# Recurrent heads of a one-core transformer kernel: level products in adjacent pairs, a second pair of decay buffers, and a new order of work on three engines

## The chip, the cores and the metric

One Trainium2 core runs the whole program. The metric is the device time of one execution in microseconds. TensorE (PE) does the matrix products, VectorE (DVE) and ScalarE (ACT) the elementwise work, GpSimd (POOL) a part of it, SyncE (SP) issues the weight transfers.

## The reference

Two blocks follow each other on one sequence of 512 tokens and width 1024: a block of two attention layers, then one layer that mixes three branches and ends in a feed-forward part. The change lies in one branch of that mixing, four recurrent heads of 128 channels:

```
q = silu(q_raw) * 128**-0.5;  f = sigmoid(f_raw);  k = 1 - f;  v = i_in      (lb is zero here)
S_t = diag(f_t) S_{t-1} + k_t v_t^T          o_t = S_t^T q_t
o = rmsnorm(o) * w * silu(g_raw)
```

It is computed chunk by chunk. Beside it run a sparse attention branch (done before) and a causal depthwise convolution of 31 taps over 2 x 128 channels, followed by a layer norm over channels and a silu. The three results are multiplied by `w_out`; then come norm and feed-forward.

## The kernel before, in words

Everything is held transposed, 128 channels on the partitions and 512 tokens along the free axis. Each engine has its own program order, written out by hand; an engine runs its list in order and waits on semaphores. A projection is a "unit": a 1024x128 weight, split by ACT into a high part `wH` (L2278) and by POOL or DVE into a low part `wL` (L632), then eight tiles of three 512-column matmuls (L1068, L1069, L1070). These units fill PE between the small products of the heads.

The four heads t = 0 to 3 go through four windows. While head t is worked on, PE computes the units of gate and value for t and of forget and query for t+1 (`fill`, `gemm_h`), in the last window the output units (`output_m`). The unit index of the first output unit is UOM, and `split_h(n)` makes the high (ACT) or low (POOL) part of a unit a few ahead of PE.

Inside a 128-token chunk the decayed product of queries and keys is built from levels. DVE multiplies a running power of the decay onto queries and keys (`raise_q` L3188, then `raise_both(t, n)`, n = 1 to 7, L3196), each time on one half of the blocks of 2^(n-1) tokens, in place in one pair of rows of `kd` (`raised`). After each raise PE computes `product(t, p)`: 64x64 products of 128-deep queries and keys (L1900; p = 7 is L1896) into PSUM banks S[0] and T[1] in turn, and DVE merges them under a mask into `aT` (`joined(t, p)`, L3206 and L3207). `product(t, p)` with p over 2 waits for `joined(t, p - 2)`, and a raise waits for the product that reads what it overwrites.

Between heads: `turn_ke` transposes the keys (L1907), ACT copies them (`take_ke` L2622), `updates` makes the state updates (L1924), DVE chains them (`states_of` L3213, L3216), and `outputs` (L1933 with the merged products, L1937 with the states) gives the head's output in PSUM. `sum_h` (L1947) sums the squares that ACT takes (`square_h`); then `root_h` on ACT, `rooted_h`, `normed_h`, `gated_h`, `low_h` on DVE finish the head and split it for the output units.

The next head's start is a chain over three engines: ACT `queries(t)` (three functions on the query unit), DVE `queries_1`, ACT `silu_scalar_2(act, "hq", t, ...)` (L1087 on `kraw`), DVE `queries_2` (L3118), DVE `raise_q` (L3188), PE `product(t, 0)`. DVE must also have `clamped(t)` and `powers(t)` (L3173, L3180) behind it, which start from ACT's `factor(t)` (L2575).

The convolution's 62 terms are scaled by ACT (`terms`, L2499, three buffers) and added by POOL (`add_terms`, L670); each waits for the other. `CONV_HEAD` says how many pairs of them each window has. `conv_sum` on PE waits for the last one. While the heads finish, DVE also reduces four blocks of a modulation matrix (`ada_block`, L1185), two buffers deep: SP loads block n+2 once block n is reduced. They stand in DVE's list ahead of `rooted_h(3)`, and the last tile of the output units (`output_m(n, (3,))`) waits for `low_h(3)`:

```
silu_z(3)
blocks(0, 1)
states_of(3)
silu_vector_2(dve, "h", 3, zraw[:, :], zsig, mark("h_gated", 3))
blocks(1, 4)
rooted_h(3)
```

## Time and profile before

| | us |
|---|---|
| median of 3 runs (1186.29 to 1187.64) | 1187.64 |
| the profiled execution, its own time | 1187.51 |
| its span, first to last instruction | 1185.7 |

The profile gives for each engine its busy time and each instruction's start and length. A row of the timeline is start, length, engine, line, operation, output<-input, count, and in brackets the idle time before it with what ended it. The heads lie at 674 to 803 us of the span: head 0's first level product starts at 673.86, those of heads 1, 2 and 3 at 698.83, 731.14 and 768.60. The recorded length of a matmul includes its pipeline, so starts are compared, not ends.

### The profile page before, as it was taken

How to read it: one execution, taken by the hardware profiler on the slowest of the kernel's cores; microseconds unless marked ns; L12 is line 12 of the kernel's file. 1: busy time of each engine (PE TensorE's matmuls, PEld its weight loads, DVE VectorE, ACT ScalarE, POOL GpSimd, SP SyncE). 2: the span in 40 equal slices, each digit the busy share in tenths (PEclk: the TensorE clock that was granted, in tenths of full speed). 3: DMA queues.
4: the chain of work that ended last, by engine and by line, in shares of the span. 5: the costliest groups of instructions: out<-in, count | busy, mean ns of one | idle time of the engine just before them, and what ended most of it. 6: DMA issues, size and time to landing. Idle time of an engine off the chain costs nothing. (4 is left out here: it accounts for less than half of the span.)

```text
span 1185.7 us, 19704 instructions
## 1 busy us (share of the span) xinstructions
PE 1170.4 (99%) x7070; PEld 961.6 (81%) x7070; DVE 804.4 (68%) x1838; ACT 690.7 (58%) x1344; POOL 457.5 (39%) x300
## 2 busy tenths in 40 slices
PE   9999999999999999999999999999999999999998
PEld 8777777777877887789677777778988889899897
DVE  6867777775777877766589766886761375475575
ACT  6766676675546778734467888754541353443542
POOL 0301111112520000053477688315454577666663
PEclk9999999999999999999999999999999999999999
DMA  5423254451543323352322112333453324223322
GB/s 203 161 72 107 92 175 142 161 160 49 200 116 117 107 90 107 107 162 70 102 68 90 37 55 72 124 101 113 131 190 106 107 71 136 82 103 108 107 72 71
DMA packets 41041, 131.82 MB, mean 111 GB/s; under 512 B 4577, under 2 KB 7265, under 8 KB 40945
## 3 DMA queue, kind: packets, MB, share of 16 engines
q1 hardware_dynamic: 35360, 121.39, 32.0%
q10 hardware_dynamic: 5584, 9.18, 2.4%
q8 instruction: 57, 0.93, 0.3%
q14 instruction: 40, 0.32, 0.1%
HBM read 127.10 MB, written 2.13 MB: 109 GB/s over the span
## 5 line engine op out<-in xcount | busy, mean ns | idle before, releaser
L1068 PE MATMUL G<-hi,wH 128*128 128x512 f32 x1032 | 417.3, 404 | 1.1 <-DVE qkv L3118 0.5
L1070 PE MATMUL G<-hi,wL 128*128 128x512 f32 x1032 | 403.1, 391 | 0.0
L1069 PE MATMUL G<-lo,wH 128*128 128x512 f32 x1032 | 402.4, 390 | 0.0
L632 POOL TENSOR_TENSOR wL<-w,wH 128x1024 fp32r<-128x1024 f32 x89 | 220.3, 2483 | 431.7 <-ACT wH L2278 428.4
L1068 PEld LDWEIGHTS G<-hi,wH 128*128 128x128 f32 x1032 | 193.8, 188 | 56.2 <-issue 17.9
L1070 PEld LDWEIGHTS G<-hi,wL 128*128 128x128 f32 x1032 | 193.7, 188 | 42.1
L1069 PEld LDWEIGHTS G<-lo,wH 128*128 128x128 f32 x1032 | 194.1, 188 | 38.3 <-issue 1.9
L2278 ACT ACTIVATE wH<-w 128x1024 fp32r<-128x1024 f32 x140 | 147.2, 1054 | 105.3 <-DMA w<-weights_dram 56.1
L417 POOL TENSOR_TENSOR kd<-kd,band 128x256 f32<-128x256 f32 x8 | 6.4, 796 | 192.8 <-DMA kd<-c_dram 192.8
L2852 DVE TENSOR_TENSOR wL<-w,wH 128x1024 fp32r<-128x1024 f32 x51 | 62.3, 1221 | 15.5 <-ACT wH L2278 15.4
L1185 DVE CUSTOM_DVE_ANT_0 adaw<-adaw,scr 128x1024 f32<-128x1024 f32 x36 | 62.5, 1737 | 0.0
L1222 ACT ACTIVATE scr<-scr,sa 128x256 f32<-128x256 f32 (+2 forms) x64 | 35.2, 557 | 22.7 <-DVE sa L1209 22.7
L2744 ACT ACTIVATE pieceH<-O 128x512 fp32r<-128x512 f32 x22 | 13.2, 599 | 58.0 <-DVE N L3389 38.0
L2779 ACT ACTIVATE relu<-G 128x512 f32<-128x512 f32 x24 | 14.3, 597 | 49.4 <-PE G L1070 49.4
L2125 PE MATMUL G<-sumH,pieceL 128*128 128x256 f32 x132 | 37.4, 283 | 0.0
L2123 PE MATMUL G<-sumH,pieceH 128*128 128x256 f32 x132 | 37.4, 283 | 0.0
L2124 PE MATMUL G<-sumL,pieceH 128*128 128x256 f32 x132 | 37.3, 283 | 0.0
L3408 DVE SCALAR_TENSOR_TENSOR xT<-G,modT,xT 128x256 f32<-128x256 f32 x44 | 21.2, 481 | 22.3 <-PE G L2125 22.1
L3196 DVE TENSOR_TENSOR kd<-kd,S 128x512 f32<-128x512 f32 x28 | 19.2, 686 | 23.9 <-PE T L1900 13.0
L710 POOL TENSOR_TENSOR pieceL<-wp,pieceH 128x512 fp32r<-128x512 f32 x18 | 25.3, 1408 | 11.8 <-ACT pieceH L2744 11.4
L1139 DVE TENSOR_TENSOR sg<-zraw,th 128x512 f32<-128x512 f32 x16 | 11.1, 692 | 26.4 <-ACT th L1087 26.4
L1245 ACT ACTIVATE scr<-T 128x384 f32<-128x384 f32 (+1 forms) x48 | 22.6, 522 | 10.9 <-PE T L1234 10.2
(565 smaller groups left out, 2569.6 us busy)
## 6 DMA issues: line engine op xcount, KB each, us to landing
w<-weights_dram SPq DMA_DIRECT2D x150, 512.0 KB, 3.6
adaw<-ada_dram SPq DMA_DIRECT2D x48, 512.0 KB, 4.4
wp<-weights_dram SPq DMA_DIRECT2D x20, 512.0 KB, 4.4
kd<-c_dram ACTq DMA_DIRECT2D x16, 512.0 KB, 5.2
xT<-x_dram SPq DMA_DIRECT2D x4, 512.0 KB, 8.1
out_dram<-xT SPq DMA_DIRECT2D x8, 256.0 KB, 2.2
scr<-ca_dram SPq DMA_DIRECT2D x2, 512.0 KB, 6.1
kd<-cbias SPq DMA_DIRECT2D x8, 128.0 KB, 4.3
```

Source lines behind the costliest of these rows:

```text
L632: g.tensor_tensor(wL[:, u.slot], raw_home(u), wH[:, u.slot].bitcast(f32), ALU.subtract).then_inc(w_lo, 1)
L710: g.tensor_tensor(pieceL[:, piece(q, i)], home, pieceH[:, piece(q, i)].bitcast(f32), ALU.subtract).then_inc(piece_lo_g, 1)
L1068: mm(home[:, :], whi, H[:, k, :], start=(k == first), stop=False)
L1069: mm(home[:, :], whi, L[:, k, :], start=False, stop=False)
L1070: last = mm(home[:, :], wlo, H[:, k, :], start=False, stop=(k == final))
L1185: v.tensor_tensor_reduce(out=home, in0=home, in1=copy, scale=1.0, scalar=0.0, op0=ALU.mult, op1=ALU.add, accum_out=modsum[:, b.n:b.n + 1]) ...
L1222: s.activation(part, part, ACT.Exp, bias=sa[:, n % 2, LOW, h, q:q + 1], scale=-1.0, accum_out=sa[:, n % 2, ASUM, h, q:q + 1]).then_inc(sem ...
L2123: mm(home, pieceH[:, at, k, :], high, start=first and k == 0, stop=False, skip_group_check=True)
L2124: mm(home, pieceH[:, at, k, :], low, start=False, stop=False, skip_group_check=True)
L2125: last = mm(home, pieceL[:, at, k, :], high, start=False, stop=(k == 3), skip_group_check=True)
L2278: s.activation(wH[:, u.slot], raw_home(u), ACT.Copy).then_inc(w_hi, 1)
L2852: v.tensor_tensor(wL[:, u.slot], w32[:, u.slot % 2], wH[:, u.slot].bitcast(f32), ALU.subtract).then_inc(w_lo, 1)
```

## The change

- Level products 3 and 4, and 5 and 6, stand next to each other in PE's list, with all of the filling between the pairs; `turn_ke(t)` follows `product(t, 7)` directly instead of opening the next window.
- `raised(t, n)` gives a second pair of rows of `kd` for n = 4, 5 and 8. The raise that goes from one pair to the other writes only its half of the blocks; ACT copies the other half (`leave(t, n)` for n = 3, 5, 7, twelve copies in all). Products 4 and 6, raises 4 and 6 and `turn_ke` wait for these copies; raises 3, 5 and 7 no longer wait for a product.
- The convolution's pairs are 3, 8, 4, 0 instead of 4, 8, 3, 0. On ACT, one pair of each window's terms is put between `queries(t)` and the query's sigmoid for t = 1 and 2.
- DVE does `states_of(t - 1)` before `queries_1(t)`, and `states_of(3)` before `silu_z(3)` and the first modulation block. The last window has a list of its own on ACT and DVE. The two `conv_scaled` of head 2's window move into head 3's.

```diff
--- before.py
+++ after.py
-CONV_HEAD = [4, 8, 3, 0]
+CONV_HEAD = [3, 8, 4, 0]
...
+AFTER.update({"h_moved": ("c_here0", 64)})
...
-def raised(t):
-
-    return kd[:, 2 - 2 * (t % 2), :], kd[:, 3 - 2 * (t % 2), :]
-
-def moved_on(t, m):
-
-    q = raised(t)[0]
+def raised(t, n):
+
+    row = 2 - 2 * (t % 2) + (4 if n in (4, 5, 8) else 0)
+    return kd[:, row, :], kd[:, row + 1, :]
+
+def moved_on(t, m, n):
+
+    q = raised(t, n)[0]
     return bass.AP(q.tensor, q.offset + m, [list(q.ap[0]), [SEQ - m, 2], [2 * m, SEQ // (2 * m)], [1, m]])
+
+def left_behind(t, m, n):
+
+    q = raised(t, n)[0]
+    return bass.AP(q.tensor, q.offset, [list(q.ap[0]), [SEQ + m, 2], [2 * m, SEQ // (2 * m)], [1, m]])
...
+        if p in (4, 6):
+            pe.wait_ge(*mark("h_moved", 3 * t + p // 2 - 1))
...
         gemm_h(1, 0, (3, 4))
         product(0, 2)
         turn_h(0)
-        gemm_h(1, 0, (5,))
+        gemm_h(1, 0, (5, 6, 7))
         product(0, 3)
-        gemm_h(1, 0, (6, 7))
         product(0, 4)
-        gemm_h(1, 1, (0, 1))
+        gemm_h(1, 1, (0, 1, 2, 3))
         product(0, 5)
-        gemm_h(1, 1, (2, 3))
         product(0, 6)
-        gemm_h(1, 1, (4, 5))
+        gemm_h(1, 1, (4, 5, 6))
         product(0, 7)
-        gemm_h(1, 1, (6, 7))
+        turn_ke(0)
+        gemm_h(1, 1, (7,))
 
     def opened(t):
 
-        turn_ke(t - 1)
         fill(t, 0)
         updates(t - 1)
         fill(t, 1)
...
 
         opened(t)
         fill(t, 3)
+        fill(t, 4, (0, 1))
         product(t, 3)
+        product(t, 4)
         if t == 2:
             conv_sum()
-        fill(t, 4)
-        product(t, 4)
+        fill(t, 4, (2, 3))
         fill(t, 5)
         product(t, 5)
+        product(t, 6)
         if t == 2:
             conv_sqsum()
         fill(t, 6)
-        product(t, 6)
         fill(t, 7, (0, 1))
         product(t, 7)
+        turn_ke(t)
         fill(t, 7, (2, 3))
 
     def last_window():
 
         opened(3)
-        fill(3, 3, (0, 1))
+        fill(3, 3)
         product(3, 3)
-        fill(3, 3, (2, 3))
         product(3, 4)
         output_m(0, (4, 5))
+        output_m(1, (4, 5))
         product(3, 5)
-        output_m(1, (4, 5))
         product(3, 6)
         output_m(0, (0, 1))
+        output_m(1, (0, 1))
         product(3, 7)
-        output_m(1, (0, 1))
         turn_ke(3)
...
+    def leave(t, n):
+
+        m = 1 << (n - 1)
+        act.wait_ge(sem("h_x"), 8 * t + n + since("h_x"))
+        if n == 3 and t > 1:
+            act.wait_ge(sem("h_o"), t - 1 + since("h_o"))
+        s.activation(left_behind(t, m, n + 1), left_behind(t, m, n), ACT.Copy).then_inc(sem("h_moved"), 1)
...
+        leave(0, 3)
         take_hv(0)
         gate_1(0)
         conv_terms(0, 0)
-        split_h(4)
+        leave(0, 5)
         forget(1)
         conv_terms(0, 1)
-        conv_terms(0, 2)
-        conv_terms(0, 3)
+        split_h(4)
+        leave(0, 7)
+        factor(1)
+        take_first(0)
+        take_ke(0)
+        keys(1)
         take_blocks(0)
-        take_first(0)
-        keys(1)
-        factor(1)
         silu_scalar_2(act, "h", 0, zsig)
 
     def window(t):
-        take_ke(t - 1)
         queries(t)
-        if t == 1:
-            split_h(5)
+        conv_terms(t - 1, 2 if t == 1 else 7)
+        split_h(4 * t + 1)
         split_h(4 * t + 2)
         silu_scalar_2(act, "hq", t, kraw[:, :])
         conv_terms(t, 0)
         raw_h(t, 2, vraw, sem("h_vturn"), t + since("h_vturn"))
-        if t == 3:
-            for k in range(2):
-                act.wait_ge(sem("conv_z"), k + 1)
-                silu_scalar_1(act, link, "cv", k, cacc[:, k, :], cv_th[k])
         conv_terms(t, 1)
         square_h(t - 1)
         conv_terms(t, 2)
-        if t == 3:
-            for k in range(2):
-                silu_scalar_2(act, "cv", k, cv_th[k])
-            for k in range(2):
-                act.wait_ge(sem("cv_gated"), k + 1)
-                s.activation(hi1[:, 6 + k, :], cv_th[k], ACT.Copy).then_inc(sem("cv_gated_hi"), 1)
+        leave(t, 3)
         conv_terms(t, 3)
         take_hv(t)
         root_h(t - 1)
         conv_terms(t, 4)
         raw_h(t, 3, zraw, sem("h_silu"), t + since("h_silu"))
         gate_1(t)
+        leave(t, 5)
         conv_terms(t, 5)
         split_h(4 * t + 3)
         if t == 2:
             for k in range(2):
                 act.wait_ge(sem("conv_centred"), k + 1)
                 s.activation(csq[:, k, :], cacc[:, k, :], ACT.Square).then_inc(sem("conv_sq"), 1)
+        forget(t + 1)
+        leave(t, 7)
+        split_h(4 * t + 4)
         gated_h(t - 1)
-        if t < 3:
-            forget(t + 1)
-        split_h(4 * t + 4)
-        if t < 3:
-            silu_scalar_2(act, "h", t, zsig)
+        silu_scalar_2(act, "h", t, zsig)
         conv_terms(t, 6)
         if t == 2:
             act.wait_ge(sem("conv_sqsum"), 1)
             rsqrt_scalar(link, 1, 1.0 / 256, sem("conv_var"), sem("conv_root"))
-        if t < 3:
-            keys(t + 1)
-            factor(t + 1)
+        factor(t + 1)
+        take_first(t)
+        take_ke(t)
+        keys(t + 1)
         take_blocks(t)
-        take_first(t)
-        conv_terms(t, 7)
-        if t < 3:
-            split_h(4 * t + 5)
+
+    def conv_gate_1(k):
+        act.wait_ge(sem("conv_z"), k + 1)
+        silu_scalar_1(act, link, "cv", k, cacc[:, k, :], cv_th[k])
+
+    def last_window():
+        queries(3)
+        split_h(13)
+        split_h(14)
+        silu_scalar_2(act, "hq", 3, kraw[:, :])
+        raw_h(3, 2, vraw, sem("h_vturn"), 3 + since("h_vturn"))
+        conv_gate_1(0)
+        square_h(2)
+        conv_gate_1(1)
+        leave(3, 3)
+        take_hv(3)
+        root_h(2)
+        raw_h(3, 3, zraw, sem("h_silu"), 3 + since("h_silu"))
+        for k in range(2):
+            silu_scalar_2(act, "cv", k, cv_th[k])
+        leave(3, 5)
+        for k in range(2):
+            act.wait_ge(sem("cv_gated"), k + 1)
+            s.activation(hi1[:, 6 + k, :], cv_th[k], ACT.Copy).then_inc(sem("cv_gated_hi"), 1)
+        gate_1(3)
+        split_h(15)
+        leave(3, 7)
+        take_first(3)
+        take_ke(3)
+        take_blocks(3)
+        gated_h(2)
+        split_h(16)
 
     attend_c()
     first_window()
-    for t in range(1, 4):
+    for t in range(1, 3):
         window(t)
-    take_ke(3)
+    last_window()
...
-        dve.wait_ge(sem("h_products"), 8 * t + (2 if n == 1 else n + 1) + since("h_products"))
+        if n in (1, 2, 4, 6):
+            dve.wait_ge(sem("h_products"), 8 * t + (2 if n == 1 else n + 1) + since("h_products"))
+        if n in (4, 6):
+            dve.wait_ge(*mark("h_moved", 3 * t + n // 2 - 1))
         dve.wait_ge(sem("h_x"), 8 * t + n + since("h_x"))
         by = power(m).rearrange("p (n a) -> p a n", a=2).unsqueeze(3).broadcast_to((P, 2, SEQ // (2 * m), m))
-        v.tensor_tensor(moved_on(t, m), moved_on(t, m), by, ALU.mult).then_inc(sem("h_x"), 1)
+        v.tensor_tensor(moved_on(t, m, n + 1), moved_on(t, m, n), by, ALU.mult).then_inc(sem("h_x"), 1)
...
-        level_of(0, 2)
+        raise_both(0, 2)
+        raise_both(0, 3)
+        joined(0, 2)
         low_c(dve, 0)
-        level_of(0, 3)
+        raise_both(0, 4)
+        joined(0, 3)
+        raise_both(0, 5)
+        joined(0, 4)
+        gates(1)
+        raise_both(0, 6)
+        raise_both(0, 7)
+        joined(0, 5)
+        joined(0, 6)
         low_c(dve, 1)
-        for n in range(4, 7):
-            level_of(0, n)
-        raise_both(0, 7)
-        gates(1)
         silu_z(0)
 
     def conv_root():
...
         for b in range(first, last_):
             ada_block(dve, Block(ADA_OM, b), 48)
 
-    def window(t):
+    def opened(t):
         clamped(t)
         powers(t)
+        states_of(t - 1)
         queries_1(t)
-        states_of(t - 1)
         queries_2(t)
         raise_q(t)
         silu_vector_2(dve, "h", t - 1, zraw[:, :], zsig,
                       mark("h_gated", t - 1) if t > 1 else (sem("a_gated_lo"), 10))
+        if t == 3:
+            conv_scaled(0)
         raise_both(t, 1)
         joined(t, 0)
         joined(t, 1)
         if t == 3:
-            for k in range(2):
-                silu_vector_1(dve, "cv", k, cacc[:, k, :], cv_th[k])
-        level_of(t, 2)
-        if t == 3:
-            conv_gate()
-        level_of(t, 3)
-        if t == 3:
-            conv_low()
-            level_of(t, 4)
+            conv_scaled(1)
+        raise_both(t, 2)
+        raise_both(t, 3)
+        joined(t, 2)
+
+    def window(t):
+        opened(t)
         rooted_h(t - 1)
-        if t < 3:
-            normed_h(t - 1)
+        raise_both(t, 4)
+        joined(t, 3)
         if t == 2:
             conv_centre()
-        level_of(t, 5 if t == 3 else 4)
-        if t == 3:
-            normed_h(t - 1)
+        raise_both(t, 5)
+        joined(t, 4)
+        normed_h(t - 1)
+        silu_z(t)
+        raise_both(t, 6)
+        raise_both(t, 7)
+        joined(t, 5)
+        joined(t, 6)
         gated_h(t - 1)
-        if t < 3:
-            silu_z(t)
-        level_of(t, 6 if t == 3 else 5)
+        gates(t + 1)
         low_h(t - 1)
-        if t < 3:
-            gates(t + 1)
-            level_of(t, 6)
         if t == 2:
             conv_root()
-        raise_both(t, 7)
-        if t == 2:
-            for k in range(2):
-                conv_scaled(k)
+
+    def last_window():
+        opened(3)
+        for k in range(2):
+            silu_vector_1(dve, "cv", k, cacc[:, k, :], cv_th[k])
+        raise_both(3, 4)
+        joined(3, 3)
+        raise_both(3, 5)
+        joined(3, 4)
+        conv_gate()
+        rooted_h(2)
+        raise_both(3, 6)
+        joined(3, 5)
+        raise_both(3, 7)
+        conv_low()
+        joined(3, 6)
+        normed_h(2)
+        gated_h(2)
+        low_h(2)
 
     logits_c(dve, 4)
     logits_c(dve, 5)
...
     gate_c(dve, 0)
     gate_c(dve, 1)
     first_window()
-    for t in range(1, 4):
+    for t in range(1, 3):
         window(t)
+    last_window()
+    states_of(3)
     silu_z(3)
     blocks(0, 1)
-    states_of(3)
     silu_vector_2(dve, "h", 3, zraw[:, :], zsig, mark("h_gated", 3))
     blocks(1, 4)
     rooted_h(3)
```

## Rows read from the trace of the kernel before

**Rows 1.** The page: span and busy time of PE.
```profile
span 1185.7 us, 19704 instructions
...
PE 1170.4 (99%) x7070; PEld 961.6 (81%) x7070; DVE 804.4 (68%) x1838; ACT 690.7 (58%) x1344; POOL 457.5 (39%) x300
```

**Rows 2.** Busy time by stretch: length, PE, PEld, DVE, ACT, POOL, clock, DMA.
```profile
707.00:728.50 21.50, 21.44 (x154) 16.48 (x153) 14.50 (x31) 21.14 (x37) 19.40 (x14) 1.00 0.17 50
731.00:768.60 37.60, 35.83 (x255) 26.80 (x254) 26.10 (x54) 25.84 (x43) 17.12 (x11) 1.00 0.37 121
```

**Rows 3.** Timeline of PE around one level product between filling matmuls.
```profile
707.35 0.39 PE L1070 MATMUL G<-hi,wL 128*128 128x512 f32 x1
707.67 0.69 PE L1900 MATMUL T<-kd 128*64 128x64 f32 x16
708.28 0.50 PE L1068 MATMUL G<-hi,wH 128*128 128x512 f32 x1
708.62 0.39 PE L1069 MATMUL G<-lo,wH 128*128 128x512 f32 x1
```

**Rows 4.** Timeline of PE at the starts of heads 1 to 3 and later.
```profile
696.61 1.05 PE L1933 MATMUL O<-scr,qkv 128*128 128x128 f32 x8
...
698.83 0.69 PE L1900 MATMUL T<-kd 128*64 128x64 f32 x16 [0.50 <-DVE kd L3188]
...
731.14 0.69 PE L1900 MATMUL T<-kd 128*64 128x64 f32 x16
...
740.59 1.98 PE L1953 MATMUL N<-tmp,ones 128*128 128x512 f32 x4
...
764.88 1.05 PE L1933 MATMUL O<-scr,qkv 128*128 128x128 f32 x8
...
768.60 0.69 PE L1900 MATMUL T<-kd 128*64 128x64 f32 x16 [0.45 <-DVE kd L3188]
...
770.02 0.39 PE L1069 MATMUL G<-lo,wH 128*128 128x512 f32 x1
...
790.79 1.05 PE L1933 MATMUL O<-scr,qkv 128*128 128x128 f32 x8
...
792.27 0.48 PE L1068 MATMUL S<-hi,wH 128*128 128x512 f32 x1
...
802.35 0.40 PE L1068 MATMUL G<-hi,wH 128*128 128x512 f32 x1
```

**Rows 5.** Timeline of ACT: both query sigmoids, and the value copy of head 1.
```profile
696.64 0.61 ACT L1087 ACTIVATE kraw<-kraw 128x512 f32<-128x512 f32 x1
...
707.04 0.58 ACT L2640 ACTIVATE qkv<-T 128x512 f32<-128x512 f32 x1
...
728.45 0.61 ACT L1087 ACTIVATE kraw<-kraw 128x512 f32<-128x512 f32 x1
```

**Rows 6.** Timeline of POOL: two low splits, the last addition, one low split.
```profile
726.55 4.78 POOL L632 TENSOR_TENSOR wL<-w,wH 128x1024 fp32r<-128x1024 f32 x2
...
737.17 1.28 POOL L670 TENSOR_TENSOR tmp<-tmp,sq 128x511 f32<-128x511 f32 x1
...
785.50 2.39 POOL L632 TENSOR_TENSOR wL<-w,wH 128x1024 fp32r<-128x1024 f32 x1 [0.35 <-ACT wH L2278]
```

**Rows 7.** Timeline of DVE from the gate of head 3 to its low part.
```profile
786.22 2.22 DVE L1082 SCALAR_TENSOR_TENSOR scr<-zraw,scr 128x512 f32<-128x512 f32 x1
788.37 1.22 DVE L1185 CUSTOM_DVE_ANT_0 adaw<-adaw,scr 128x1024 f32<-128x1024 f32 x1
...
791.18 1.22 DVE L1185 CUSTOM_DVE_ANT_0 adaw<-adaw,scr 128x1024 f32<-128x1024 f32 x1
...
796.69 1.23 DVE L1185 CUSTOM_DVE_ANT_0 adaw<-adaw,scr 128x1024 f32<-128x1024 f32 x1
...
797.84 0.69 DVE L781 SCALAR_TENSOR_TENSOR sq<-sq,scr 128x512 f32<-128x512 f32 x1
...
801.45 0.69 DVE L3233 TENSOR_TENSOR lo<-O,hi 128x512 fp32r<-128x512 f32 x1 [0.67 <-ACT hi L2617]
```

More of the change, by code:

```diff
@@ L1891, in product @@
                     pe.wait_ge(sem("h_aT"), 7 * t + p - 1 + since("h_aT"))
-                q, k = raised(t)
+                q, k = raised(t, max(p, 1))
                 out_ = half_of(p)
@@ L1904, in turn_ke @@
                 pe.wait_ge(sem("h_x"), 8 * t + 8 + since("h_x"))
+                pe.wait_ge(*mark("h_moved", 3 * t + 3))
                 pe.wait_ge(sem("h_v"), t + 1 + since("h_v"))
                 for c in range(3):
-                    last = nc.tensor.transpose(T[0][:, c * P:(c + 1) * P], raised(t)[1][:, c * P:(c + 1) * P], ident[:, :])
+                    last = nc.tensor.transpose(T[0][:, c * P:(c + 1) * P], raised(t, 8)[1][:, c * P:(c + 1) * P], ident[:, :])
                 last.then_inc(sem("h_keT"), 1)
@@ L1936, in outputs @@
                 for c in range(1, NQ):
-                    last = mm(O[:, c * P:(c + 1) * P], state[:, c - 1, :], raised(t)[0][:, c * P:(c + 1) * P], start=False,
+                    last = mm(O[:, c * P:(c + 1) * P], state[:, c - 1, :], raised(t, 8)[0][:, c * P:(c + 1) * P], start=False,
                               stop=(c == NQ - 1))
@@ L2593, in keys @@
                     act.wait_ge(sem("h_keT"), t - 1)
-                s.activation(raised(t)[1], klog, ACT.Exp, scale=-1.0).then_inc(sem("h_k"), 1)
+                s.activation(raised(t, 1)[1], klog, ACT.Exp, scale=-1.0).then_inc(sem("h_k"), 1)
             def queries(t):
@@ L3187, in raise_q @@
                     dve.wait_ge(sem("h_o"), t - 1 + since("h_o"))
-                v.tensor_tensor(raised(t)[0], power(1), hq, ALU.mult).then_inc(sem("h_x"), 1)
+                v.tensor_tensor(raised(t, 1)[0], power(1), hq, ALU.mult).then_inc(sem("h_x"), 1)
             def raise_both(t, n):
                 m = 1 << (n - 1)
-                dve.wait_ge(sem("h_products"), 8 * t + (2 if n == 1 else n + 1) + since("h_products"))
+                if n in (1, 2, 4, 6):
+                    dve.wait_ge(sem("h_products"), 8 * t + (2 if n == 1 else n + 1) + since("h_products"))
+                if n in (4, 6):
+                    dve.wait_ge(*mark("h_moved", 3 * t + n // 2 - 1))
                 dve.wait_ge(sem("h_x"), 8 * t + n + since("h_x"))
                 by = power(m).rearrange("p (n a) -> p a n", a=2).unsqueeze(3).broadcast_to((P, 2, SEQ // (2 * m), m))
-                v.tensor_tensor(moved_on(t, m), moved_on(t, m), by, ALU.mult).then_inc(sem("h_x"), 1)
+                v.tensor_tensor(moved_on(t, m, n + 1), moved_on(t, m, n), by, ALU.mult).then_inc(sem("h_x"), 1)
             def joined(t, p):
```

## The prediction

> **What bounds the kernel now.** I read the page first: PE is busy 1170.4 of 1185.7 us [rows 1], so only PE's order and its few idle stretches can be worth anything, and the whole kernel has about 15 us of idle PE. Next the timeline of PE through the heads, from start to start. It is one unbroken stream of filling matmuls with small work between, with gaps mainly where a new head opens [rows 4]: from the start of the merged-product outputs to the first level product 2.22 us pass for head 1 and 3.72 us for head 3, while the same stretch of the last head, where nothing waits, takes 1.48 us. The stall is 0.7 us at head 1 and 2.2 us at head 3. Then ACT: between its value copy of head 1 and the query sigmoid of head 2 it is busy 21.14 of 21.50 us [rows 2, 5]. In that window ACT, not PE, has no room. In the next one (731 to 768.6) ACT is busy only 25.8 of 37.6 us. Last the tail: the tile of the output units that needs the last head starts at 802.35 [rows 4], and the low part that it needs was begun at 801.45 and takes 0.69 us [rows 7], so it ended at 802.14. PE arrives there just as it is ready. Any earlier arrival of PE is worth nothing unless that chain comes earlier too.
>
> **Adjacent products.** PE gets no instruction more or less. A lone product costs 708.62 - 707.35 = 1.27 us from filling matmul to the second one after it; two filling steps of 0.23 us would have passed anyway, which leaves 0.81 us [rows 3]. The pair of head 3 takes 1.42 us from its start to the second filling matmul [rows 4]; less one step of 0.23, plus the 0.09 of entry that the lone one shows, 1.28 us. A merge saves 0.34 us. There are eight, 2.7 us; the transposes beside product 7 I put at under 0.1 us each. With the two stalls above and some tenths at head 1's transposes the ceiling is some 6 to 7 us, if nothing new waits.
>
> **The copies on ACT.** No row shows one. The nearest is the same engine's 128x512 from SBUF to SBUF, 0.61 us [rows 5]; as they read and write in steps it could be more, but hardly over twice that, and because consecutive instructions overlap by a tenth it could be 0.5. I take 0.6. In the first window they and one dropped pair of terms nearly cancel (three copies 1.8, a pair 1.2), so head 1 opens near 698.3, and ACT's value copy of head 1 stays at about 707.1, since before it ACT and POOL pace each other through the convolution terms and POOL's list is no shorter. From there to the query sigmoid of head 2 is 728.45 - 707.04 = 21.4 us of solid work. The new order has the same work there (the pair of terms and the high splits of the next units stand in front of the sigmoid in both) and two copies more: 707.15 + 21.4 + 1.2 = 729.75. From the sigmoid to product 0 it takes 698.83 - 696.64 = 2.2 us (head 2 took 2.7) [rows 4, 5]. Product 0 of head 2 comes at 732.0, against 731.14: 0.8 us later, though PE could be there at about 729.6. What the merges of two windows gave, and the stalls of the first, turns into a wait for the query chain. Behind it on PE stands everything else.
>
> **Head 2's window.** Product 0 to product 0 of head 3 was 37.46 us. Off go the stall 2.24 and two merges 0.7: `conv_scaled` (two operations per half) no longer stands ahead of the powers on DVE, and the states come ahead of the queries. On comes a wait for the convolution: POOL does one pair of terms more ahead of its two low splits, which began at 726.55 [rows 6] and now follow the terms that ACT computes only after `queries(2)`, so about 729.6; after them come two additions of up to 1.28 more. The last addition ended at 738.45 and will end at 738.45 + 3.1 + 2 x 1.28 = 744.1. `conv_sum` stood at 740.59; it moves by 0.8, six filling steps (1.4) and a second product (0.5) to 743.3, and waits 0.8. Head 3 opens at 732.0 + 37.46 - 2.24 - 0.7 + 0.8 = 767.3, against 768.60. If ACT or POOL are quicker than I think, 766.
>
> **The last window and its tail.** PE saves two merges more and would reach the last tile at 802.35 - 1.3 - 0.7 = 800.3. But the tail is later. DVE's new list ends with raise 6, joined 5, raise 7, two `conv_low`, joined 6, `normed_h(2)`, `gated_h(2)`; `rooted_h(2)` holds raise 6 to about 782.0, and with steps of 0.6 (0.35 for a joined, 0.8 and 0.7 for the last two) `gated_h(2)` ends at 786.6. ACT's high copy takes 0.6, `low_h(2)` 0.6, and then `states_of(3)` 1.05 stands ahead of the gate: `silu_z(3)` is due at 788.9. ACT goes from that high copy into the high split of 16 (1.04 us) and POOL's low split follows, about 788.2 to 790.6. This is the moment that decides. In the trace `silu_z(3)` took 2.22 us and ended at 788.44, 0.55 us after the low split that ran on POOL from 785.50 to 787.89 [rows 6, 7]; both its inputs are in SBUF. So it is held again, to 791.2. The first modulation block starts at 791.1 instead of 788.37. From its start to the end of the second were 4.03 us, now 2.95, as the states no longer lie between: 794.05 instead of 792.40. SP may load the fourth only then, and it takes 4.29 us to be there (796.69 - 792.40): 798.35; 1.15 us on, `rooted_h(3)` starts at 799.5 instead of 797.84. Its chain to the low part is unchanged, so the last tile starts at about 804.0, 1.7 us later than before, with PE idle for some 3.7 us in front of it. Behind 803 us everything follows that tile.
>
> The Trainium skill, "SBUF — State Buffer", section Who interferes with whom, says that a VectorE instruction with two inputs in SBUF and a GpSimd instruction that reads SBUF exclude each other, and the one that comes second waits for the whole of the first. By that rule, which the 2.22 us agree with, the gate is held; without it the first block starts at 789.5, `rooted_h(3)` at 797.9, and the sum is no change.
>
> **The sum.** The profiled execution took 1187.51 us for its span of 1185.7, 0.1 from the median of 1187.64. Heads 0 and 1 +0.8, head 2's window -2.1, last window -0.7, tail +3.7: 1.7 us, so 1187.64 + 1.7 = 1189.3 us. A measurement of this kernel can tell about 0.2%, 2.4 us, from no change.
>
> **Rivals.**
> - *A second hold in the last window (slower).* `conv_low(1)`, whose inputs are both in SBUF, is due at 784.1; the low split of 15 starts on POOL at 784.1 too (`conv_gate` done 780.6, then copy 0.5, gate 1.85, split 1.04). If POOL is first, DVE loses 2.3 us; `output_m(0, (6, 7))` on PE waits for it and the tail starts 2.3 later: 1191.6 us. It decides from one or two tenths on. For it: the tie. Against it: a tenth of delay on ACT undoes it. Chance 0.20.
> - *The gate is not held (no change).* If the low split of 16 starts after 788.9 or is over, the tail comes as before, 1187.7 us. Against it: both times hang on the same high copy and lie 0.7 us apart. Chance 0.15.
> - *PE's arrival decides (faster).* If the low part of the last head is ready by 800.3, the gain is 2.0 us, 1185.6; without the wait for `conv_sum` and with head 2's sigmoid a microsecond sooner, 1183.8. For it: the two stalls do go. Against it: the chain of two buffers of 4.3 us per load is in DVE's list ahead of `rooted_h(3)` in both kernels. It needs the first block to start by 787.4. Chance 0.23.
> - My forecast, 0.42.
>
> **How the numbers follow.** The forecast's own range is 1.7 +- 1 us, as window 2 can come out 1.3 us earlier and a copy can cost 0.5 to 1 us: 1188.3 to 1190.5. A quarter of it lies over 2.4 us. Slower by over 0.2%: 0.20 + 0.10 = 0.30. Faster by over 0.2%: three quarters of the third rival, 0.18. The rest 0.52 within. The range runs from the third rival's far end to the first's: 1184.0 to 1191.8; I leave out 0.1 on either side.
>
> **What the profile after would show.** Products 3 and 4, 5 and 6 with 0.5 us from start to start; twelve copies on ACT of about 0.6; product 0 of head 2 not earlier than 731 with an idle PE in front of it, released by DVE's raise; product 0 of head 3 near 767.3; no stall on the states; `conv_sum` behind POOL's last addition; `silu_z(3)` over 2 us long; a PE idle for 2 to 4 us before the last tile, behind `low_h(3)`. I am wrong if head 2 opens at 730 (then ACT had room), if head 3 opens before 765.5, or if the last tile starts within 0.5 us of 800.3.

## The result, and the profile after

The changed kernel takes 1190.22 us (median of 11 runs, 1188.25 to 1193.19) against 1187.64 for the kernel before (11 runs, 1184.55 to 1189.97): ratio over all runs 1.003, 95% interval 1.002 to 1.0041 (the two medians alone give 1.0022). Forecast were 1189.3. It is slower, in the direction of the forecast: by 2.6 us between the medians where 1.7 were forecast, and by some 3.6 us, twice the forecast, by the ratio.

The page of the changed kernel, next to [rows 1]: PE has 3.3 us less busy time in a span that is 2.6 us longer.

```profile
span 1188.3 us, 19706 instructions
...
PE 1167.1 (98%) x7070; PEld 961.0 (81%) x7070; DVE 803.2 (68%) x1838; ACT 695.7 (59%) x1356; POOL 458.9 (39%) x300
```

The best single reading is one window, from head 0's first level product to the start of the last tile. Columns as in [rows 2]. First the kernel before:

```profile
673.86:802.35 128.49, 125.94 (x959) 96.56 (x959) 92.05 (x192) 95.16 (x158) 72.67 (x48) 1.00 0.27 83
```

then the changed one:

```profile
673.44:804.81 131.37, 122.70 (x959) 96.63 (x959) 91.12 (x192) 100.39 (x170) 73.07 (x48) 1.00 0.25 81
...
707.15:729.93 22.78, 22.03 (x162) 17.81 (x161) 14.85 (x32) 22.45 (x38) 17.57 (x13) 1.00 0.16 47
732.11:767.70 35.59, 34.92 (x254) 26.75 (x254) 22.20 (x49) 27.28 (x46) 21.16 (x14) 1.00 0.32 108
```

PE does the same 959 matmuls in 3.24 us less busy time. That is what PE's new order gives, the adjacent products foremost (no run takes them apart from the rest of the order). Its idle time in the stretch goes from 128.49 - 125.94 = 2.55 us to 8.67. So 6.12 us of new idle time stand against 3.24 us of gain: 2.88 us longer. From the last tile on, both kernels are alike: 383.35 us to the end of the span before, 383.49 after. The start of the stretch lies anywhere from 670.5 to 673.9 us in the twelve profiled executions, one of each kernel, for reasons that lie ahead of the heads. So from here on I count from head 0's first product.

Where the idle time is, timeline of PE:

```profile
698.37 0.69 PE L1909 MATMUL T<-kd 128*64 128x64 f32 x16 [1.64 <-DVE kd L3226]
...
703.97 1.12 PE L1957 MATMUL N<-sq,ones 128*128 128x512 f32 x2 [0.26 <-ACT sq L2618]
...
709.15 0.69 PE L1909 MATMUL T<-kd 128*64 128x64 f32 x16
709.66 0.64 PE L1909 MATMUL S<-kd 128*64 128x64 f32 x16
710.23 0.50 PE L1075 MATMUL G<-hi,wH 128*128 128x512 f32 x1
710.57 0.39 PE L1076 MATMUL G<-lo,wH 128*128 128x512 f32 x1
...
716.66 0.50 PE L1075 MATMUL G<-hi,wH 128*128 128x512 f32 x1 [0.60 <-DVE scr L1089]
...
732.11 0.69 PE L1909 MATMUL T<-kd 128*64 128x64 f32 x16 [0.92 <-DVE kd L3226]
...
744.42 1.98 PE L1963 MATMUL N<-tmp,ones 128*128 128x512 f32 x4 [0.32 <-POOL tmp L677]
...
767.70 0.69 PE L1909 MATMUL T<-kd 128*64 128x64 f32 x16
...
792.91 1.13 PE L1957 MATMUL N<-sq,ones 128*128 128x512 f32 x2 [1.48 <-ACT sq L2618]
...
804.81 0.50 PE L1075 MATMUL G<-hi,wH 128*128 128x512 f32 x1 [2.59 <-DVE lo L3274]
```

Read the brackets against [rows 4]. All brackets of the stretch, with three that are not shown (0.35, 0.16 and 0.35), add up to the 8.67 us. The pair (709.15, 709.66) costs 1.42 us to the second filling matmul, as forecast. The stalls ahead of head 3 (1.28 on the states, in the row of the kernel before below, and 0.45 on the raise) are gone. New are 1.64 ahead of head 1 (was 0.50), 0.60 on DVE's gate at 716.66, 0.92 ahead of head 2 (was none), 1.48 at `sum_h(3)` and 2.59 at the last tile.

```profile
767.22 0.94 PE L1937 MATMUL O<-kd,scr 128*128 128x128 f32 x6 [1.28 <-DVE scr L3216]
```

ACT ahead of head 2 (compare [rows 5]): the copy, the value copy of head 1, two high splits, the query's sigmoid.

```profile
705.58 0.62 ACT L2639 ACTIVATE kd<-kd 128x512 f32<-128x512 f32 x1
...
707.63 0.58 ACT L2657 ACTIVATE qkv<-T 128x512 f32<-128x512 f32 x1
...
728.04 1.99 ACT L2287 ACTIVATE wH<-w 128x1024 fp32r<-128x1024 f32 x2
729.93 0.61 ACT L1094 ACTIVATE kraw<-kraw 128x512 f32<-128x512 f32 x1
```

POOL in the windows of heads 2 and 3 (compare [rows 6]):

```profile
730.09 5.17 POOL L639 TENSOR_TENSOR wL<-w,wH 128x1024 fp32r<-128x1024 f32 x2
...
743.10 1.27 POOL L677 TENSOR_TENSOR tmp<-tmp,sq 128x511 f32<-128x511 f32 x1
...
784.45 2.90 POOL L639 TENSOR_TENSOR wL<-w,wH 128x1024 fp32r<-128x1024 f32 x1 [16.09 <-ACT wH L2287]
788.80 2.36 POOL L639 TENSOR_TENSOR wL<-w,wH 128x1024 fp32r<-128x1024 f32 x1 [1.45 <-ACT wH L2287]
```

DVE in the tail (compare [rows 7]): second `conv_low`, `silu_z(3)`, the four blocks, `rooted_h(3)`, `low_h(3)`.

```profile
784.42 0.69 DVE L3304 TENSOR_TENSOR lo<-rinv,hi 128x512 fp32r<-128x512 f32 x1
...
789.24 2.47 DVE L1089 SCALAR_TENSOR_TENSOR scr<-zraw,scr 128x512 f32<-128x512 f32 x1
791.64 1.21 DVE L1192 CUSTOM_DVE_ANT_0 adaw<-adaw,scr 128x1024 f32<-128x1024 f32 x1
...
793.39 1.21 DVE L1192 CUSTOM_DVE_ANT_0 adaw<-adaw,scr 128x1024 f32<-128x1024 f32 x1
...
797.87 1.22 DVE L1192 CUSTOM_DVE_ANT_0 adaw<-adaw,scr 128x1024 f32<-128x1024 f32 x1
...
799.31 1.23 DVE L1192 CUSTOM_DVE_ANT_0 adaw<-adaw,scr 128x1024 f32<-128x1024 f32 x1
...
800.46 0.69 DVE L788 SCALAR_TENSOR_TENSOR sq<-sq,scr 128x512 f32<-128x512 f32 x1
...
804.06 0.69 DVE L3274 TENSOR_TENSOR lo<-O,hi 128x512 fp32r<-128x512 f32 x1 [0.66 <-ACT hi L2626]
```

Put the last two fences beside each other. POOL starts the low split of unit 16 at 788.80, DVE starts the gate at 789.24, and the gate ends 2.47 us later, at 791.71, half a microsecond after the split (791.16). The earlier pair is the near miss of the second rival: DVE started `conv_low(1)` at 784.42, POOL its split at 784.45. DVE was first by 0.03 us, ran its normal 0.69, and POOL took 2.90 in place of 2.36 to 2.41.

### The profile page after: what moved, and what is told of

It is laid out like the page before. It is cut to its first block, busy times and chain, and to the rows that moved or that the text cites. A ratio compares the mean times of both kernels' runs of the same rounds, so it can differ in the third digit from the quotient of the medians.

```text
span 1188.3 us, 19706 instructions
## 1 busy us (share of the span) xinstructions
PE 1167.1 (98%) x7070; PEld 961.0 (81%) x7070; DVE 803.2 (68%) x1838; ACT 695.7 (59%) x1356; POOL 458.9 (39%) x300
## 4 chain that ended last, share of the span: by engine, by line
PE 54%; DVE 7%; issue 7%; POOL 3%; ACT 2%; DMA 2%; SPq 0%; ACTq 0%; DVEq 0%; POOLq 0%
PE G L1075 10%; PE G L1077 10%; PE G L1076 10%; DMA adaw<-ada_dram 2%; PE G L2132 2%; PE G L2134 2%; PE G L2133 2%; POOL wL L639 2%; DVE best L3202 1%; DVE adaw L3204 1%; PE S L1426 1%; PE T L1473 1%; PE O L1489 1%; POOL pieceL L717 1%; POOL tmp L677 1%
## 5 line engine op out<-in xcount | busy, mean ns | idle before, releaser
L3471 DVE SCALAR_TENSOR_TENSOR xT<-G,modT,xT 128x256 f32<-128x256 f32 x44 | 21.2, 482 | 22.3 <-PE G L2134 22.0
L1216 DVE CUSTOM_DVE_ANT_0 scr<-S,kd 128x256 f32<-128x256 f32 (+2 forms) x64 | 28.5, 487 | 0.0
```

## The experiments

Ten kernels ran. Each number in the table is from the one profiled execution of its kernel and counts from head 0's first product (those of `e1` and `e9` were the slowest of all runs of their kernel, that of `e2` the fastest); "idle" is PE's idle time right before the last tile, "rest" the time from that tile's start to the end of the span.

| kernel | head 1 | head 2 | head 3 | last tile | idle | rest |
|---|---|---|---|---|---|---|
| before | 24.97 | 57.28 | 94.74 | 128.49 | 0 | 383.4 |
| changed | 24.93 | 58.67 | 94.26 | 131.37 | 2.59 | 383.5 |
| e1_tail_order | 24.94 | 58.67 | 94.26 | 133.07 | 0 | 383.2 |
| e2_gate_early | 24.94 | 58.68 | 94.27 | 130.77 | 3.44 | 383.4 |
| e3_copies_twice | 24.94 | 60.35 | 96.50 | 133.79 | 2.75 | 384.9 |
| e4_sigmoid_earlier | 24.26 | 57.73 | 94.28 | 131.16 | 2.35 | 383.5 |
| e5_blocks_early | 24.92 | 58.66 | 94.27 | 127.15 | 0 | 383.3 |
| e6_before_blocks_early | 24.99 | 57.31 | 94.80 | 128.57 | 0 | 383.3 |
| e7_both | 24.26 | 57.73 | 94.26 | 127.99 | 0 | 383.6 |
| e8_conv_sum_later | 24.25 | 57.72 | 93.92 | 127.66 | 0 | 383.3 |
| e9_split_16_short | 24.92 | 58.66 | 94.25 | 130.22 | 2.91 | 385.1 |
| e10_windows_1_2 | 24.23 | 57.70 | 93.89 | 126.81 | 0 | 383.6 |

### e1: the tail's order as before

```diff
     last_window()
-    states_of(3)
     silu_z(3)
     blocks(0, 1)
+    states_of(3)
```

> The changed kernel with the gate of head 3 and the first modulation block ahead of states_of(3), as before. My theory (the tail decides: the gate is held behind POOL's low split): the gate is issued before POOL starts, takes 0.7 instead of 2.47 us, the first block starts 2.7 us earlier, the outputs of head 3 wait 1.3 us for the states, the fourth block lands 1.6 us earlier and the last tile of the output units starts 1.6 us earlier. Total about 1188.6 us, 0.13% under the changed kernel. Rival (the tail is set by PE's arrival or by the transfers alone): no change from the changed kernel, 1190.2.

Measured 1189.58 us, ratio 1.0025 (1.0015 to 1.0036). The gate was indeed not held (0.68 us), but what came next was. All engines, in order of time:

```profile
788.24 0.68 DVE L1089 SCALAR_TENSOR_TENSOR scr<-zraw,scr 128x512 f32<-128x512 f32 x1
788.76 2.37 POOL L639 TENSOR_TENSOR wL<-w,wH 128x1024 fp32r<-128x1024 f32 x1 [1.45 <-ACT wH L2287]
788.85 3.37 DVE L1192 CUSTOM_DVE_ANT_0 adaw<-adaw,scr 128x1024 f32<-128x1024 f32 x1
```

The first block takes 3.37 us for 1.21. The states behind it are late, and PE waits 3.22 us for them:

```profile
793.25 1.65 PE L1947 MATMUL O<-kd,scr 128*128 128x128 f32 x6 [3.22 <-DVE scr L3257]
```

TensorE's granted clock falls to 0.50 of full speed within that wait, at about 792 us, and stays there until 799; filling matmuls start every 0.42 us in place of 0.23. The last tile is 1.7 us later than in the changed kernel. The last head's low part on DVE and the tile on PE tell what of this is the tail:

```profile
804.49 0.69 DVE L3274 TENSOR_TENSOR lo<-O,hi 128x512 fp32r<-128x512 f32 x1 [0.67 <-ACT hi L2626]
...
806.47 0.39 PE L1075 MATMUL G<-hi,wH 128*128 128x512 f32 x1
```

Counted from head 0 the low part starts at 131.09, 0.47 us later than in the changed kernel (130.62). The other 1.2 us are PE, which comes after the low part is ready: from the outputs with the states to the tile it takes 13.22 us, and in the changed kernel, without its two waits, 10.84. So some 2.4 us are the low clock. My expectation was wrong: the hold had moved to another instruction, and the tail was no shorter for it. One order keeps the states early and the gate held, the other frees the gate and holds the block. Without the low clock PE would have been at the tile before the low part, and the tile some 0.5 us later and not 1.7. The times of all runs do not show the loss: the ratio is 1.0025 here and 1.003 for the changed kernel.

### e2: the gate ahead of `low_h(2)`

```diff
     gated_h(2)
+    silu_z(3)
     low_h(2)
     ...
     states_of(3)
-    silu_z(3)
```

> The changed kernel with silu_z(3) between gated_h(2) and low_h(2), where DVE is idle for 0.8 us. My theory: the gate takes 0.7 us, states_of(3) keep their time, the first block starts 2.4 us earlier, and the last tile too: PE idle in front of it falls from 2.6 us to about 0.3. Total about 1187.8 us, level with the kernel before. Rival (the loads of the blocks decide, and they stand on SP behind the load that waits for POOL's low split of 16, at 791.2): the third block lands no earlier than 795.6 and the fourth with it, and the gain is 1 us or less. Rival (PE's arrival decides): no gain.

Measured 1189.53 us, 1.0025 (1.0015 to 1.0036). The gate, at 783.82, takes 1.15 us. Again the hold passes on, all engines:

```profile
785.86 2.37 POOL L639 TENSOR_TENSOR wL<-w,wH 128x1024 fp32r<-128x1024 f32 x1 [1.45 <-ACT wH L2287]
786.45 2.86 DVE L1192 CUSTOM_DVE_ANT_0 adaw<-adaw,scr 128x1024 f32<-128x1024 f32 x1
```

The first block ends 0.6 us earlier than in the changed kernel (counted from head 0), and so does the last tile. The gate started 2.5 us earlier, and only 0.6 of it was left once block 0 had met the split. PE's idle time before the tile rose to 3.44 us where I had expected 0.3, since PE no longer waits at `sum_h(3)` and comes sooner.

### e3: three copies of head 1 done twice

```diff
     s.activation(left_behind(t, m, n + 1), left_behind(t, m, n), ACT.Copy)
+    if t == 1:
+        link(s.activation(left_behind(t, m, n + 1), left_behind(t, m, n), ACT.Copy))
```

> The changed kernel with each of the three copies of head 1 done twice on ACT, the second after the first has ended (about 0.65 us each). My theory (ACT has no room in head 1's window): two of the three extra copies lie behind the value copy, and product 0 of head 2 comes 1.3 us later, with PE idle in front of it; head 3 and the last tile follow by about the same, 1.3 us, total 1191.5. Rival (the copies are hidden in ACT's idle time): no change in the place of product 0 of head 2.

Measured 1192.65 us, 1.0048 (1.0031 to 1.0065). A second copy takes 0.65 us, and three of them move head 2 by 1.68 us, head 3 by 2.24, the last tile by 2.42. Two of them, 1.3 us, lie behind the value copy, which itself comes 0.4 us later. ACT has no room before head 2, and what is lost there is not won back. The further 0.56 us at head 3 are not the copies alone: behind the 2.23 us that PE waits ahead of head 2 the granted clock is 0.50 from 734 to 737.5 us, which this expectation did not foresee.

### e4: the query's sigmoid ahead of the second high split

```diff
     split_h(4 * t + 1)
-    split_h(4 * t + 2)
     silu_scalar_2(act, "hq", t, kraw[:, :])
+    split_h(4 * t + 2)
```

> The changed kernel with the query sigmoid of heads 1 and 2 ahead of the second of the two high splits on ACT. My theory: product 0 of head 1 comes 0.7 us and that of head 2 about 0.95 us earlier after head 0's first product, but conv_sum waits for POOL's last addition that much longer, so head 3 opens at most 0.2 us earlier and the total is unchanged within 0.3 us. Rival (the query chain is the only brake): head 3, the last tile and the total come 0.9 us earlier.

Measured 1188.53 us, 1.0019 (1.0007 to 1.003). Heads 1 and 2 open 0.67 and 0.94 us earlier, head 3 at the same time (+0.02), the last tile 0.21 earlier. The start of heads 1 and 2 hangs on ACT's order, as forecast. The run shows too that an earlier head 2 alone is worth nothing: PE then waits 1.31 us for `sum_h(1)` (0.35 in the changed kernel) and 0.35 for the last addition.

### e5 and e6: blocks out of the tail, in both kernels

`e5` puts the first two blocks into DVE's idle time in the last window, loads blocks 2 and 3 ahead of the last two of the output units that SP loads there, and takes the gate ahead of `low_h(2)`:

```diff
     for k in range(2):
         silu_vector_1(dve, "cv", k, cacc[:, k, :], cv_th[k])
+    blocks(0, 2)
     raise_both(3, 4)
     ...
     gated_h(2)
+    silu_z(3)
     low_h(2)
     ...
     states_of(3)
-    silu_z(3)
-    blocks(0, 1)
     silu_vector_2(dve, "h", 3, ...)
-    blocks(1, 4)
+    blocks(2, 4)
     rooted_h(3)
...
-    for n in range(5):
+    for n in range(3):
         load_unit(Unit(UOM + 1 + n))
-    for b in range(2, 6):
+    for b in range(2, 4):
+        load_ada(Block(ADA_OM, b))
+    for n in range(3, 5):
+        load_unit(Unit(UOM + 1 + n))
+    for b in range(4, 6):
         load_ada(Block(ADA_OM, b))
```

> The changed kernel with the first two modulation blocks in DVE's idle time before raise_both(3, 4), the loads of the next two ahead of the output units' last two loads on SP, and silu_z(3) ahead of low_h(2). My theory (the last tile waits for a chain that the blocks lengthen): rooted_h(3) starts when its root is there, low_h(3) ends about 4 us earlier, PE no longer idles before the last tile, which starts 127.3 us after head 0's first product (131.37 in the changed kernel, 128.49 before). Total 1.2 us under the kernel before: ratio 0.999. Rival (the loss is the query chain and the copies, the blocks only fill a wait): the last tile stays at 130 or later, ratio over 1.001.

Measured 1183.94 us, ratio 0.9981 (0.997 to 0.9993). DVE of `e5`: the first block, the gate, the multiplication by the gate, `rooted_h(3)`.

```profile
774.21 1.22 DVE L1196 CUSTOM_DVE_ANT_0 adaw<-adaw,scr 128x1024 f32<-128x1024 f32 x1
...
785.52 1.15 DVE L1093 SCALAR_TENSOR_TENSOR scr<-zraw,scr 128x512 f32<-128x512 f32 x1
...
788.34 2.02 DVE L1150 TENSOR_TENSOR sg<-zraw,scr 128x512 f32<-128x512 f32 x1
...
793.85 0.69 DVE L792 SCALAR_TENSOR_TENSOR sq<-sq,scr 128x512 f32<-128x512 f32 x1 [1.19 <-ACT sq L787]
```

The edit has three parts, the blocks, the loads and the gate; only the gate was tried alone (`e2`). A hold still happens (2.02 for 0.68), but now it costs nothing: `rooted_h(3)` waits 1.19 us for its root. The stretch's own window:

```profile
672.06:799.21 127.15, 122.47 (x959) 96.81 (x960) 90.82 (x192) 100.34 (x170) 73.04 (x48) 1.00 0.26 84
```

The last tile comes 4.22 us earlier than in the changed kernel, 1.34 earlier than before. `e6` asks whether that is only the blocks. It takes the first block out of the tail of the kernel before, with the same order of loads:

```diff
     if t == 3:
         conv_gate()
+        blocks(0, 1)
...
     silu_z(3)
-    blocks(0, 1)
     states_of(3)
```

> The kernel before with its first modulation block in DVE's idle time in the last window and the loads of the next two moved ahead in the same way. My theory: before, PE's arrival and the low part of the last head coincide, so an earlier low part alone is worth nothing: the last tile stays at 128.5 after head 0's first product, ratio 1.000. Rival (the blocks held the kernel before as well): last tile 0.5 us or more earlier.

Measured 1186.12 us, 0.9999 (0.9989 to 1.0009), last tile at 128.57. But this edit shortens the tail by very little: the gate is still held (2.22 us), the last block still waits for its load, and the low part starts at 127.23 after head 0 where it had 127.59. What says that a shorter tail is worth nothing there is PE itself, which is idle for 0 us before the tile in both kernels and would reach it at 128.5 in any case. That the two edits are worth something only together is read from this, and not measured with a tail that is as short as in `e5`.

### e7, e8 and e10: both cures

`e7` is `e5` with the sigmoid of `e4` earlier for all three heads. `e8` adds `conv_sum` after two more filling steps and `conv_centre` one raise later. `e10` is `e8` with the last window's ACT list left as in `e5`.

```diff
     def last_window():           (ACT; e7 and e8, not e10)
         queries(3)
         split_h(13)
-        split_h(14)
         silu_scalar_2(act, "hq", 3, kraw[:, :])
+        split_h(14)
...
-        if t == 2:               (PE; e8 and e10)
-            conv_sum()
         fill(t, 4, (2, 3))
+        if t == 2:
+            conv_sum()
...
-        if t == 2:               (DVE; e8 and e10)
-            conv_centre()
         raise_both(t, 5)
         joined(t, 4)
+        if t == 2:
+            conv_centre()
```

> e5 with the query sigmoid of heads 1 to 3 ahead of the second high split. My theory: heads 1 and 2 open at 24.3 and 57.7 after head 0's first product, head 3 at 94.2, since conv_sum waits for POOL's last addition whatever PE does; the last tile as in e5, at most 0.3 us earlier. Rival (the query chain is the only brake left): head 3 and the last tile 0.9 us earlier than in e5.

> e7 with conv_sum two filling tiles later on PE and conv_centre after joined(2, 4) on DVE. My theory: conv_sum waits no more and the pair of products 5 and 6 comes 0.9 us earlier, but the squares, the root and the powers of head 3 on ACT and DVE come later by about 1 us, so head 3 opens between 93.5 and 94.5 and the total moves by less than 0.5 us from e7. Rival (the wait for POOL was the brake): head 3 opens at 93.3 and the last tile 0.9 us earlier than in e7.

Measured 1184.65 us (0.999, 0.998 to 1.0) and 1184.34 (0.9989, 0.9978 to 1.0001). The heads open earlier as expected, but the last tile comes 0.84 us (`e7`) and 0.51 us (`e8`) later than in `e5` and not earlier. The multiplication by the gate as head 3 opens tells why. DVE of `e7`:

```profile
764.80 2.50 DVE L1150 TENSOR_TENSOR sg<-zraw,scr 128x512 f32<-128x512 f32 x1
```

Counted from head 0 it starts at the same time as in `e5` (93.86 and 93.88), since the sigmoid of head 3 waits for DVE and not for ACT. But in `e5` it takes 1.59 us:

```profile
765.94 1.59 DVE L1150 TENSOR_TENSOR sg<-zraw,scr 128x512 f32<-128x512 f32 x1
```

The edit had only pushed ACT's high split of 14 behind the sigmoid, and with it POOL's low split, whose end moves from 94.9 to 95.8 after head 0's first product. So the multiplication is held 0.9 us longer, and PE waits 0.52 us at `sum_h(2)`. `e10` takes back that one move, and keeps the rest of `e8`.

> e5_blocks_early with two edits in the windows of heads 1 and 2 alone: the query's sigmoid ahead of the second high split, and conv_sum of head 2's window after the last two filling steps of part 4 (conv_centre one raise later). The last window's ACT list stays that of e5. Theory (e7_both lost 0.85 us only because head 3's earlier sigmoid brought DVE's gate beside POOL's low splits): heads 1, 2 and 3 open at 24.26, 57.72 and 93.92 after head 0's first product, gated_h at the opening of head 3 takes 1.6 us and not 2.5, and the last tile comes 32.9 after head 3 opens, at 126.8, against 127.15 of e5_blocks_early and 127.99 of e7_both. Whole about 0.35 us under e5_blocks_early, which cannot be told from it by time. Rival (the earlier heads themselves cost it): last tile at 127.6 or later.

Measured 1183.62 us, 0.997 (0.9958 to 0.9983). DVE of `e10`, and below it its stretch:

```profile
764.86 1.61 DVE L1150 TENSOR_TENSOR sg<-zraw,scr 128x512 f32<-128x512 f32 x1
```

```profile
671.36:798.17 126.81, 122.44 (x959) 96.80 (x959) 92.36 (x192) 100.68 (x170) 73.08 (x48) 1.00 0.27 84
```

The heads and the last tile stand within 0.03 us of what was expected. This version beats the kernel before by 0.3%. The last tile, 1.68 us earlier, accounts for 0.14%; the interval begins at 0.17%. The mean granted clock of each run points at the rest: it averages 0.9987 over the runs of `e10` and 0.9979 over the runs of the kernel before that were taken with them, and the runs of the two that have the same mean clock, 0.999, take 1183.4 and 1185.2 us, 1.8 us apart where the tile has 1.68. That fewer waits of PE are the reason for the higher mean is likely, but no run shows it.

### e9: the low split of unit 16 cut short

```diff
-    g.tensor_tensor(wL[:, u.slot], raw_home(u), wH[:, u.slot].bitcast(f32), ALU.subtract)
+    g.tensor_tensor(wL[:, u.slot, 0, 0:4], raw_home(u)[:, 0, 0:4], wH[:, u.slot, 0, 0:4].bitcast(f32), ALU.subtract)
```

> The changed kernel with the low split of unit 16 on POOL cut to 4 of its 1024 columns (so the output units that read that weight's low part use old values), which leaves the order of all lists as it is and takes away only the 2.4 us in which POOL reads SBUF beside silu_z(3). Theory (the gate was held by the split, and the tail hangs on the gate): silu_z(3) takes 1.15 us where it took 2.47, the first block starts 1.3 earlier, and so do the loads of the third and fourth, rooted_h(3) and the last tile, 130.05 after head 0's first product where the changed kernel has 131.37; PE's idle time before it 1.3 where it was 2.6; whole 1.3 us less. Rival (the tail hangs on something else, on PE or ACT): the last tile stays at 131.4, or moves by under 0.3.

Measured 1189.76 us, 1.0015 (1.0002 to 1.0029). DVE of `e9`, gate and first block:

```profile
789.70 0.68 DVE L1096 SCALAR_TENSOR_TENSOR scr<-zraw,scr 128x512 f32<-128x512 f32 x1
790.32 1.22 DVE L1199 CUSTOM_DVE_ANT_0 adaw<-adaw,scr 128x1024 f32<-128x1024 f32 x1
```

With nothing else changed in the order of work, the gate's 2.47 us became 0.68 (not 1.15: that figure of other runs held part of a wait too: in `e2` the gate ends at 114.49, 0.56 us after POOL's split of 15), and the last tile moved from 131.37 to 130.22: the hold and its worth at the last tile, 1.15 us of the 1.79 that the gate won, are shown. Two more things I had wrong. First, PE's idle time before the tile did not shrink, since `sum_h(3)` no longer waited 1.48 us (that wait was the held gate too, through ACT's square), and PE came sooner as well. Second, the 1.15 us were lost again behind the tile. PE of `e9`:

```profile
804.13 0.79 PE L1082 MATMUL G<-hi,wH 128*128 128x512 f32 x1 [2.91 <-DVE lo L3281]
804.72 0.63 PE L1083 MATMUL G<-lo,wH 128*128 128x512 f32 x1
805.14 0.63 PE L1084 MATMUL G<-hi,wL 128*128 128x512 f32 x1
...
807.39 0.39 PE L1084 MATMUL S<-hi,wL 128*128 128x512 f32 x1
```

Matmuls start every 0.43 us for nearly 3 us, at a granted clock of 0.50, and "rest" is 385.1; all other kernels but `e3` (384.9) have 383.2 to 383.6.

## Why the prediction was right, and where it was off

**What bounds the kernel now.** Right. PE had no idle time before the last tile, and so met the tail exactly; in `e6` a low part that is 0.36 us earlier moves nothing. The two stalls that I put at 0.7 and 2.2 us from starts have 0.50 and 1.28 + 0.45 = 1.73 us in the profile's brackets.

**Adjacent products.** Right in kind, a little low: 3.24 us of PE's busy time where I had 2.7 and something under 0.1 for each of the four transposes. It is the sum over the whole new order: 1.32, 0.40, 0.81 and 0.71 us in the four windows, so not the same for each pair, and no run parts the pairs from the transposes.

**The copies on ACT.** A copy takes 0.62 us on the mean of the twelve (forecast 0.6). The sigmoid of head 2 came at 729.93 (forecast 729.75), `product(2, 0)` at 732.11 (732.0), released by DVE's raise, PE idle in front of it. Yet the shift was sized wrongly: head 0 began 0.42 us earlier in this execution, so the +0.8 was really +1.39. What failed is the step that "ACT's value copy of head 1 stays at about 707.1": counted from head 0 it came 1.0 us later (34.19 after 33.18). I had held that POOL's list is no shorter and paces ACT as before. But POOL adds the pair of terms that was put ahead of head 1's sigmoid before its two low splits: these start 22.85 us after head 0's first product (22.02 before) and take 5.18 us (4.70), and ACT then waits 3.64 us for the additions behind them where it had waited 2.54. One copy stands in front of the value copy too. No run parts the two; the wait for POOL alone accounts for the 1.0 us. From there to the sigmoid were 22.3 us, 22.6 forecast. The 0.60 us that PE waited for DVE's gate at 716.66 I had not named; they cost nothing, as PE waited for the query chain behind it anyway. `e3` and `e4` show from both sides that head 2 hangs on what stands before its sigmoid on ACT.

**Head 2's window.** 35.59 us where 35.32 were forecast. The stall on the states is gone, `conv_sum` waits for POOL's last addition, which ended at 744.37 (744.1 forecast), by 0.32 us and not 0.8, as PE itself was late. Head 3 opened 0.48 us earlier than before, not 1.3.

**Last window and tail.** From head 3's opening I had 21.6 us to the gate, 23.8 to the first block, 32.2 to `rooted_h(3)`, 36.7 to the last tile; measured are 21.54, 23.94, 32.76 and 37.11. The held gate is right, and `e9` shows it. What was too small is the load of a block: from the end of the second block to the start of the fourth I had 4.29 us, and it was 799.31 - 794.60 = 4.71. PE's arrival was off by more, without any effect on the end. By my sum it needs 800.3 - 767.3 = 33.0 us from head 3; in `e5` and `e10`, where nothing is in its way, it needs 32.88 and 32.92. In the changed kernel 1.48 us at `sum_h(3)` came on top, which I had not named, and so the idle time at the tile was 2.59 and not 3.7. That this error did no harm is luck: the low part was later still.

So the last tile came 2.88 us later and not 1.7: 0.5 from ACT before head 2, 0.3 from head 2's window, 0.4 from the tail, all on the same side. Only the first changes the picture: the loss before head 2 is 1.39 us where I gave it 0.8. These are places in the sum and not what a cure is worth: `e4` took 0.94 us back at head 2 and the tile came 0.21 earlier, `e9` took the hold away and it came 1.15 earlier, `e5` took two blocks out of the tail, with their loads and the gate moved, and it came 4.22 earlier. The chain of blocks and loads ahead of `rooted_h(3)`, named in the third rival as what stands against it, was the costliest thing in the way.

**The hold.** Each held instruction ends about its own length after POOL's split: the gate and the multiplication 0.55 us after it, the blocks 1.1 us. So the gate takes 2.47 us against 0.68 alone, the block 3.37 and 2.86 against 1.21, the multiplication 2.50 against 0.68, and POOL itself takes 2.90 and not 2.36 when it is second. The Trainium skill's rule, "SBUF — State Buffer", section Who interferes with whom (a VectorE instruction with two SBUF inputs and a GpSimd instruction that reads SBUF exclude each other, the second waits for the first), agrees with the runs on each of them.

**The rivals.** The second hold at `conv_low(1)` missed by 0.03 us; its price was not tried. That the tie fell this way is luck for the forecast, but it is no toss between executions: in the ten profiled executions with this list DVE is first by 0.03 to 0.04 us each time, and POOL takes 2.9. "PE's arrival decides" is false for the kernel as changed, but it is exactly what `e5` and `e10` are. "The gate is not held" is false, and `e1` and `e2` show that moving the gate alone would have helped little (the low part 0.47 us later in `e1`, the tile 0.6 earlier in `e2`): with the split of 16 where it is, some instruction of DVE pays for it.

**The range.** 1189.3 + 1 is 1190.3, and not the 1190.5 that stands there; the measured median lies under both.

## What to carry to other kernels

Write down PE's busy and idle time in one window around the change, before and after: here 3.24 us of real gain stood in one column and 6.12 us of new waits in the other, and each wait named the next edit. When two engines exclude each other, moving the victim picks another victim; look for the place where DVE waits anyway and put the work there. A faster engine is worth nothing until the chain that it meets is shortened too (the changed kernel against `e5`), and where an engine without idle time meets that chain, a shorter chain alone is worth nothing either (`e6`, as far as it went).

## What I had not expected of the hardware

TensorE's granted clock fell to its lower level (1.2 of 2.4 GHz, starts 0.42 to 0.43 us apart in place of 0.23) at four waits of the heads in three runs: 3.22 us of idle PE in `e1`, 2.23 (ahead of head 2) and 2.75 in `e3`, 2.91 in `e9`. It stayed there for some 3 us, in `e1` for 7, and in the three waits of the last window it fell while PE was still idle. At the last tile it cost 1.4 (`e3`) and 1.6 us (`e9`) of "rest", in `e1` some 2.4 us of PE's way to the tile. It did not fall behind 2.59 us in the changed kernel, 2.35 in `e4` or 3.44 in `e2`. Once each it fell far ahead of the heads too, at 541 us in the kernel before and at 325 us in the changed kernel and `e9`, where the longest wait of PE in the 15 us before was 0.53, 0.36 and 0.77 us. The length of the wait alone does not decide it, and what does stays open.

In the profiled executions it explains how `e9` can have its last tile 1.15 us earlier than the changed kernel and win nothing by it. Over all runs the mean granted clock goes the same way: 0.9975 for the changed kernel, 0.9966, 0.9969, 0.9964, 0.9981 and 0.9972 for `e1`, `e2`, `e3`, `e4` and `e9`, which all wait over 2 us before the last tile or for the states, but 0.9985 to 0.9988 for `e5` to `e8` and `e10`, which do not. The kernel before has 0.998 in the batches whose clocks are on record.
